# Second softmax attention of a three-mixer block in jobs of two banks, with three 64-row score products per head

## The reference, cut

```python
def sink_softmax(s, mask, sink):
    s = jnp.where(mask, s, NEG_INF)
    m = jnp.maximum(jnp.max(s, axis=-1, keepdims=True), sink)
    e = jnp.exp(s - m)
    return e / (jnp.sum(e, axis=-1, keepdims=True) + jnp.exp(sink - m))

def swa_sink_mixer(h, positions, w_in, q_gain, k_gain, sinks, w_out):
    ...
    q, k, v, z = jnp.split(h @ w_in, np.cumsum([MIX_WIDTH, kvd, kvd]).tolist(), axis=-1)
    q = q_groups(rope(rms_norm(split_heads(q, N_HEADS), q_gain), positions), g)
    k = jnp.pad(kv_groups(rope(rms_norm(split_heads(k, g), k_gain), positions)), pad)
    ...
    o = merge_blocks(lax.map(block_fn, jnp.arange(s // Q_BLOCK)))
    return (o * jax.nn.silu(z)) @ w_out
```

## Time and profile before

| | us |
|---|---|
| median of 3 runs (lowest, highest) | 844.62 (843.43, 844.91) |
| the profiled execution | 844.54 |
| its span, first to last instruction | 842.7 |
| PE busy | 801.4 (95%) |
| DVE busy | 561.2 (67%) |
| ACT busy | 429.0 (51%) |
| POOL busy | 113.6 (13%) |
| mean granted clock of TensorE | 0.993 of full speed |

### The profile page before, as it was taken

How to read it: one execution, slowest core, us unless ns; L and a number is a source line. 1 busy time by engine, 2 the same in 40 slices (tenths; PEclk the granted TensorE clock), 3 DMA queues, 4 the chain that set the end, 5 groups by cost and what they waited for, 6 DMA issues and landing times.

```text
span 842.7 us, 13226 instructions
## 1 busy us (share of the span) xinstructions
PE 801.4 (95%) x5114; PEld 698.4 (83%) x5114; DVE 561.2 (67%) x954; ACT 429.0 (51%) x838; POOL 113.6 (13%) x108
## 2 busy tenths in 40 slices
PE   5989999998889899999999999999999999999996
PEld 4768987776789678999988988889997788888885
DVE  5896977846887855346635657775875566566665
ACT  5436647825547544446536535555444445455453
POOL 2243214501532302000000000013001000000000
PEclk9999999999989999999999999999999999999999
DMA  9745411233442235544432534333654637655541
GB/s 313 214 154 170 136 51 35 68 124 111 149 151 101 75 101 174 177 150 149 152 101 85 166 104 146 101 101 100 225 174 129 217 131 234 227 174 190 186 164 51
DMA packets 93502, 121.38 MB, mean 144 GB/s; under 512 B 8760, under 2 KB 69616, under 8 KB 93440
## 3 DMA queue, kind: packets, MB, share of 16 engines
q1 hardware_dynamic: 92432, 117.80, 43.3%
q0 software_dynamic: 432, 1.57, 0.6%
q10 hardware_dynamic: 576, 1.17, 0.4%
HBM read 119.48 MB, written 1.05 MB: 143 GB/s over the span
## 4 chain that ended last, share of the span: by engine, by line
PE 79%; DVE 12%; issue 3%; ACT 1%; POOL 1%; POOLq 0%; DVEq 0%; ACTq 0%
PE banks L415 18%; PE banks L417 17%; PE banks L416 17%; PE banks L459 8%; PE banks L461 3%; DVE w_lo L1495 3%; PE banks L561 1%; DVE small L1589 1%; PE banks L617 1%; PE banks L945 1%; PE banks L422 1%; PE banks L421 1%; PE banks L575 1%; PE banks L520 1%; PE banks L555 1%
## 5 line engine op out<-in xcount | busy, mean ns | idle before, releaser
L1495 DVE TENSOR_TENSOR w_lo<-raw,w_hi 128x1024 fp32r<-128x1024 f32 x216 | 267.6, 1248 | 113.1 <-ACT w_hi L1092 111.1
L1092 ACT CAST w_hi<-raw 128x1024 fp32r<-128x1024 f32 (+1 forms) x217 | 225.2, 1045 | 155.6 <-PE banks L417 111.5
L415 PE MATMUL banks<-h,w_hi 128*128 128x256 f32 (+1 forms) x512 | 150.0, 293 | 2.9 <-DVE w_lo L1495 2.9
L416 PE MATMUL banks<-h,w_hi 128*128 128x256 f32 (+1 forms) x512 | 146.7, 286 | 0.0
L417 PE MATMUL banks<-h,w_lo 128*128 128x256 f32 (+1 forms) x512 | 145.7, 285 | 0.0
L415 PE MATMUL banks<-w_hi,h 128*128 128x512 f32 (+1 forms) x288 | 115.5, 401 | 11.6 <-DVE w_lo L1495 6.7
L417 PE MATMUL banks<-w_hi,h 128*128 128x512 f32 (+1 forms) x288 | 113.1, 393 | 0.0
L416 PE MATMUL banks<-w_lo,h 128*128 128x512 f32 (+1 forms) x288 | 112.8, 392 | 0.0
L415 PEld LDWEIGHTS banks<-h,w_hi 128*128 128x128 f32 x512 | 97.2, 190 | 7.3 <-issue 6.4
L459 PE MATMUL banks<-h,w_hi 128*128 128x512 f32 x288 | 99.1, 392 | 0.0
L417 PEld LDWEIGHTS banks<-h,w_lo 128*128 128x128 f32 x512 | 97.8, 191 | 0.0
(11 more groups left out here) (319 smaller groups left out, 1362.9 us busy)
## 6 DMA issues: line engine op xcount, KB each, us to landing
raw<-in_w_in SPq DMA_DIRECT2D x24, 1024.0 KB, 5.2
raw<-in_a_w_in SPq DMA_DIRECT2D x14, 1024.0 KB, 5.4
raw<-in_w_ffn_gate SPq DMA_DIRECT2D x11, 1024.0 KB, 5.4
raw<-in_w_ffn_up SPq DMA_DIRECT2D x11, 1024.0 KB, 5.4
raw<-in_w_ffn_down SPq DMA_DIRECT2D x11, 1024.0 KB, 5.0
raw<-in_b_w_in SPq DMA_DIRECT2D x9, 1024.0 KB, 5.3
raw<-in_w_gate SPq DMA_DIRECT2D x8, 1024.0 KB, 5.7
raw<-in_a_w_out SPq DMA_DIRECT2D x4, 1024.0 KB, 5.1
```

What stands on the lines that cost most here:

```text
L415: mm(o, lh, rh, start=start, stop=False)
L416: mm(o, lh, rl, start=False, stop=False)
L1092: nc.scalar.copy(split(w_hi, s), rawsub(s)[0]).then_inc(S["hi_ready"], 1)
L1495: V.tensor_tensor(split(w_lo, s), rawsub(s)[0], split(w_hi, s).bitcast(F), ALU.subtract).then_inc(S["lo_ready"], 1)
```

## The change

The second attention gets a loop of its own (`wide_attention`), and the first keeps the old one.

- **Products of 64 rows.** q is no longer stored as hi above lo. `o2_hi` and `o2_lo` hold it with two heads along the 128 rows, and the key lies twice as before. Each head takes three products of 64 rows (hi.hi, lo.hi, hi.lo) in place of two of 128. The heads of a pair use rows 0 to 63 and 64 to 127 and write to the two banks of a pair of banks, in turns.
- **Jobs of two banks.** Six jobs of 1024 columns (4 heads of tile 1, 4 more, 8 heads of tile 0, and again) in place of twelve of 512. Masks go to each bank. One maximum reduces both banks; ACT copies all transposed weights, DVE none. The lag between scores and transposes is 2 jobs, to the values 3. Weights go to three buffers of 1024 columns.
- **Moved into the loop.** The transposes and splits of the second half of q (heads 8 to 15) stand in iteration 0, behind the first job's scores and z3. Iterations 0 to 3 hold z4 to z7. The sub of z0 is cast by DVE before the first half of q is split, that of z1 right behind it. The first sub of the output projection (`out_first`) stands before the last job's values; for that the first two column panels of `b_out` are swapped, and banks 2 and 3 take subs 0 and 1.

```diff
...
-    def out_panels(name, m):
+    def out_panels(name, m, first=(0, 512)):
         v = m.rearrange("(a p) n -> p a n", p=P)
         for half in range(2):
-            for c0 in (0, 512):
+            for c0 in (0, 512) if half else first:
                 add(name, v[:, 4 * half:4 * half + 4, c0:c0 + 512], 4, 512, 2, "rows")
...
+    out_panels("b_out", w["b_w_out"], (512, 0))
...
+        p_buf = [ar[:, 8192:9216], ar[:, 9216:10240], tmp[:, 0:1024]]
...
+        WIDE = [(qt, tuple(range(b, b + n))) for a in range(0, NH, 8) for qt, b, n in ((1, a, 4), (1, a + 4, 4), (0, a, 8))]
+        LAGW = 2
...
+        def z_done_wide(j):
+            return 3 + min(max(j + 1, 0), 5)
...
+        def score_banks(j):
+            return pairs[1 - j % 2]
...
+        def quads_after(j):
+            return (2 * (j // 3), 2 * (j // 3) + 1) if 0 <= j < len(WIDE) and j % 3 == 2 else ()
...
+        def tbank(phase, e):
+            return ps[(6, 7, 4, 5, 4, 5)[e] if phase else (0, 1, 2, 3, 6, 7, 4, 5, 6, 7, 4, 5)[e]]
+        def z_bank(phase, f):
+            return ps[6 + f % 2 if phase and f >= 3 else f % 2]
...
-                        pe.wait_ge(S["tq_dve"], 8 + e - 3 if phase else e - 7)
+                        pe.wait_ge(S["tq_dve"], 12 if phase else e - 7)
...
+            def wide_attention(z0, s_out):
+                n = len(WIDE)
+                def scores(j):
+                    qt, heads = WIDE[j]
+                    w = P * (qt + 1)
+                    if j == 0:
+                        pe.wait_ge(S["rp_free"], 16)
+                    elif j == 1:
+                        pe.wait_ge(S["z_free"], 11)
+                    else:
+                        pe.wait_ge(S["p_exp"], NJ + 2 * j - 2)
+                    b = score_banks(j)
+                    nb = 4 // (qt + 1)
+                    for u in range(2):
+                        rows = b[:, u, :].rearrange("p (r n) -> p r n", n=w)
+                        mm(rows[:, :, w - P:w], tri, bc(far, [P, nb, P], 1), start=True, stop=True)
+                        if qt:
+                            mm(rows[:, :, 0:P], not_after, bc(far, [P, nb, P], 1), start=False, stop=False, skip_group_check=True)
+                    for q, k in ((o2_hi, k_hi), (o2_lo, k_hi), (o2_hi, k_lo)):
+                        for i in range(len(heads) // 2):
+                            for u in range(2):
+                                h, a = heads[2 * i + u], 64 * u
+                                last = mm(b[:, u, w * i:w * i + w], q[a:a + 64, h // 2, P * qt:P * qt + P],
+                                          k[a:a + 64, h // 8, 0, 0:w], start=False, stop=k is k_lo, skip_group_check=True)
+                    last.then_inc(S["s_ready"], 1)
...
+                def transposes(j):
...
+                    for u in range(2):
+                        pe.wait_ge(S["p_ready"], NJ + 2 * j + u + 1)
+                        if j:
+                            pe.wait_ge(S["pt_sb"], pt_wide(j - 1, u))
+                        for i in range(4):
+                            last = nc.tensor.transpose(ps[4 + u][:, P * i:P * i + P], p_buf[j % 3][:, 512 * u + P * i:512 * u + P * i + P], ident)
+                        last.then_inc(S["pt_ps"], 1)
...
+                def pv(j):
+                    qt, heads = WIDE[j]
+                    quad = heads[0] // 4
+                    pe.wait_ge(S["pt_sb"], pt_wide(j, 1))
+                    if j < 2:
+                        pe.wait_ge(S["z_free"], 15 + j)
+                    elif qt and quad >= 2:
+                        pe.wait_ge(S["og_ready"], 4 + quad - 1)
+                    for i in range(len(heads) // 2):
...
+                for j in range(n + LAGW + 1):
+                    if j < n:
+                        scores(j)
+                    if j == 0:
+                        z_tiles(1, z0, 3, 4)
+                        for tt in range(2):
+                            pe.wait_ge(S["rp_out"], 13 + tt)
+                            head_transposes(4 + tt, 1, q_half(tt, 1))
+                    if j < 4:
+                        z_tiles(1, z0, 4 + j, 5 + j)
+                    if j == 1:
+                        meta_transposes()
+                    if 0 <= j - LAGW < n:
+                        transposes(j - LAGW)
+                    if j == n + LAGW:
+                        pe.wait_ge(S["p_exp"], NJ + 2 * n - 2)
+                        out_first(s_out, 0)
+                    if j > LAGW:
+                        pv(j - LAGW - 1)
+                pe.wait_ge(S["p_exp"], NJ + 2 * n)
+            def out_first(s0, q):
+                if q < 2:
+                    pe.wait_ge(S["ot_lo"], 4 + q + 1)
+                weights_ready(s0 + q)
+                for j in range(2):
+                    last = tm_half(s0 + q, j, 2 * (q % 2) + j, hx(h_hi), hx(h_lo), (2, 3) if q < 2 else (0, 1), k_last=KT)
+                last.then_inc(S["sub_used"], 1)
...
+                    if n == 2:
+                        if q:
+                            out_first(s0, q)
+                        continue
...
-            z_tiles(1, first["b_z"], 1, 2)
-            for tt in range(2):
-                pe.wait_ge(S["rp_out"], 13 + tt)
-                head_transposes(4 + tt, 1, q_half(tt, 1))
-            z_tiles(1, first["b_z"], 2, 3)
-            pe.wait_ge(S["tq_dve"], 14)
-            attention(1, first["b_z"])
-            pe.wait_ge(S["z_free"], 16)
+            z_tiles(1, first["b_z"], 1, 3)
+            pe.wait_ge(S["tq_dve"], 12)
+            wide_attention(first["b_z"], first["b_out"])
...
+            def wide_attention(z0):
+                n = len(WIDE)
+                for j in range(n + LAGW + 3):
+                    if 1 <= j < 5:
+                        z_tanh(1, z0, 3 + j)
+                    v = j - LAGW
+                    if 0 <= v < n:
+                        for u in range(2):
+                            act.wait_ge(S["pt_ps"], NJ + 2 * v + u + 1)
+                            if v >= 2 and u == 0:
+                                act.wait_ge(S["pv"], NJ + v - 1)
+                            nc.scalar.copy(xn[:, 1024 * (v % 2) + 512 * u:1024 * (v % 2) + 512 * u + 512], ps[4 + u]).then_inc(S["pt_sb"], 1)
...
+                        act.wait_ge(S["s_max"], NJ + j + 1)
+                        if j >= 3:
+                            act.wait_ge(S["pt_ps"], NJ + 2 * j - 4)
...
+                    if j == 0:
+                        z_tanh(1, z0, 3)
+                        for i in range(2):
+                            q_hi_wide(4 + i, i, 1)
+                    for q in quads_after(j - LAGW - 2):
+                        output_hi(1, q)
+                    split_hi_to(z0 + z_done_wide(j) + RING)
...
+                def maxima(j):
+                    qt, heads = WIDE[j]
+                    nb, c = 4 // (qt + 1), 8 * (j % 4)
+                    dve.wait_ge(S["s_ready"], NJ + j + 1)
+                    m = nmax[:, c:c + 2 * nb]
+                    h = heads[0]
+                    by = lambda t: t[:, h:h + 2 * nb].rearrange("p (r u) -> p u r", u=2)
+                    of = lambda t: t.rearrange("p (u r) -> p u r", u=2)
+                    link(V.tensor_reduce(m, score_banks(j)[:, :, :].rearrange("p u (r n) -> p (u r) n", r=nb), X, ALU.max, negate=True))
+                    link(V.tensor_tensor(of(m), of(m), by(nsink), ALU.min))
+                    V.tensor_tensor(of(facs[:, 32 + c:32 + c + 2 * nb]), of(m), by(sink), ALU.add).then_inc(S["s_max"], 1)
...
+                    link(V.tensor_tensor(f, facs[:, 32 + c:32 + c + 2 * nb], sm_, ALU.add))
+                    V.reciprocal(f, f).then_inc(S["p_fac"], 1)
...
+                    if 1 <= j < 5:
+                        z_gate(1, 3 + j)
+                    if j == 0:
+                        z_gate(1, 3)
+                        for i in range(2):
+                            q_lo_wide(4 + i, i, 1)
+                        dve.wait_ge(S["m_rstd"], 1)
+                        V.tensor_scalar(meta_in, meta_in, m_st[:, 2:3], None, ALU.mult).then_inc(S["m_n"], 1)
...
+                    for q in quads_after(j - LAGW - 2):
+                        output_lo(1, q)
+                    if j == n:
...
+            split_lo_to(base + 3 + RING)
             for i in range(2):
-                q_lo(i, 12, 8 + i, i, 0)
-            split_lo_to(base + 5 + RING)
+                q_lo_wide(i, i, 0)
+            split_lo_to(base + 4 + RING)
...
-            dve.wait_ge(S["m_rstd"], 1)
-            V.tensor_scalar(meta_in, meta_in, m_st[:, 2:3], None, ALU.mult).then_inc(S["m_n"], 1)
+            rope_item(14, 15, 2, 8, 4, 0, q8(0, 1), 12)
+            z_gate(1, 0)
+            split_lo_to(base + RING - 1)
...
+                key_lo(2 + i, 1, 0, i, 2)
+            rope_item(15, 16, 3, 8, 4, 1, q8(1, 1), 13)
+            split_lo_to(base + RING)
             z_gate(1, 1)
-            for i in range(2):
-                q_lo(4 + i, 12, 12 + i, i, 1)
             split_lo_to(base + 2 + RING)
```

(5 more changed lines are left out.)

415 lines of the change are left out of this document (209 added, 206 removed).

## The result

The changed kernel takes **834.87 us** (834.01 to 835.61 in 4 runs) beside 844.76 us for the kernel before in the same comparison: a ratio of 0.9879, with a 95% interval of 0.9862 to 0.9896. It is faster by 1.2%, more than the 0.2% that can be told from no change. The forecast was 833.7 us, its range 831.0 to 839.5.

A forecast was written before the change was run, and what follows sets the result against it. PE's work and waits were taken to bound the kernel; in the stage from b_q2's last sub to the output projection, 5.2 + 0.3 + 2.5 + 3.8 + 3.4 - 4.4 = 10.8 us saved, 844.5 to 833.7; range 831.0 to 839.5.

The forecast's parts named there:

- Part 1: PE's wait before gate tile z0: the earlier cast saves 2.9 us waiting, 2.3 low clock; 0.3 more for low-clock transposes.
- Part 2: Second half of q: scores and z3 cover its rope and POOL, so waits of 1.7 and 0.8 go; 2.5 us saved.
- Part 3: PE's own work in the attention jobs: paired 64-row products and wider jobs take 21.6 us instead of 25.0; 3.4 saved.
- rival of serial pairs: Scores: the 64-row pairs run one after another, costing 5.4 us on PE's path; 839.1 us, chance 0.12.
- Part 4: Loop's tail: old waits of 3.8 us go; new ones before job 1's values and job 4's and 5's transposes cost 4.4.
- The third: In the tail, the new wait of PE before the transposes of job 5: 1.6 to 2 us.
- rival of the clock in the tail: From 270 us PE's three waits lower the clock, so first output subs run at half speed: 836.7 us, chance 0.12.

The follow-up runs named there:

- e8: Changed kernel with one more wait on PE ahead of gate tile z0, about 2.8 us at the old first wait's place: 839.19 us, ratio 0.9923 to before.
- e1: Changed kernel with DVE's cast of z0 put back behind the two splits of q: 836.36 us, ratio 0.9889 to the kernel before.
- e2: Kernel before with one edit only, the cast of z0 ahead of the four splits of q: 844.52 us, ratio 0.9987 to the kernel before.
- e7: Changed kernel with PE's transposes of q's second half back ahead of the first scores and z3: 838.18 us, ratio 0.9908 to the kernel before.
- e9: Changed kernel with every 64-row score product on rows 0 to 63, number and size kept: 841.53 us, ratio 0.9950 to the kernel before.
- e4: Changed kernel with DVE's gate of z7 ahead of the maxima of job 4: 835.22 us, ratio 0.9870 to the kernel before.
- e6: Changed kernel with DVE's factors of job 4 ahead of the maxima of job 5: 835.26 us, ratio 0.9877 to the kernel before.

## Why the prediction was right, and where not

The sum was 10.8 us; the stage gave 9.0. The forecast of 833.7 started from the profiled 844.54, and the profiled execution of the changed kernel took 835.6, 1.9 more than forecast. That the median is only 1.2 off is luck in part: two of its four executions were 1.5 us shorter. The direction, the places and most sizes held:

- **Part 1**, 5.2 + 0.3: the wait and the low clock are gone, and e8's profile confirms their price. The cause was wrong in part. I credited the moved cast; e1 shows that the cheaper splits alone leave only 0.8 of it. And the term was taken as independent, which e2 refutes.
- **Part 2**, 2.5: both waits are gone, and 0.68 before z3 came instead. I had named z3 the tightest, by 0.4, but put z2's cast at its quiet price. It took 1.90 beside POOL. e7's profile prices the part at 1.9. *Mis-sized: -0.7.*
- **Part 3**, 3.4: the rival of serial pairs is out (e9). But the jobs take 23.2 us, not 21.6. Scores of tile 1 take 246.84 - 245.37 = 1.47 to 1.57 (1.4 was put), of tile 0 2.14 (2.0); six groups 10.4 instead of 9.6. The transposes take 6.45 instead of 6.0 and the values 6.3 instead of 6.0, mostly for a first instruction behind a wait or a change of form. The 0.2 that I gave the change of form was an estimate, and too little: about 0.1 each for entering (the first product starts 245.94 - 245.73 = 0.21 us behind the last mask, where masks follow each other at 0.12), for the first pair (0.38 against 0.28 us) and for leaving (247.07 - 246.84 = 0.23 to the next start, where 0.12 is the pitch). *Mis-sized: -1.6, the largest error.*
- **Part 4**, old waits -3.8, new ones +4.4: they measure 1.37 (1.3 put), 1.08 + 0.34 (1.5), 0.83 + 0.52 (1.6 to 2), with 0.12 more before the values of job 0: 4.3. Right, although e4 and e6 show that they are not three costs but one chain: shortening the first gives 0.3 us, and taking the second away gives nothing or a loss. The third was put in the sum at its low end, 1.6, where its own terms give 7.6 - 5.5 = 2.1; it measured 1.35. That the old waits are gone is seen in the profile alone: no run put DVE's copies, or the first output sub, back in their old place.
- **The rest.** Of the 1.8 us missed, -0.7 and -1.6 are named above and +0.1 is the tail's. The other +0.4 lies in gate tiles and in the transposes of q and the meta tokens, which took 25.0 us together where 25.4 was put.
- **The rival of the clock in the tail** did not come about: 1.00 from 262 to 290 us, behind waits of up to 1.37. It was nearer than I thought, since in e6's profile it did (0.50), behind 2.53 us in one piece. In the profile of e7 PE waited 2.42 us between transposes and the clock stayed at 1.00, as it did in the tail with its transposes; no run took the transposes out, so it is not shown what they do to the clock.

## To carry to other kernels

A wait that is removed is worth only what the next supplier allows: before adding two gains, put the consumer forward by the first and ask each queue behind it whether it comes forward too (e2 took 2.9 us of wait away, and the stage stayed at 65.5). In a tail whose waits hang on one chain, remove the head of that chain (here a tanh on ACT behind a cast, and the gate on DVE that uses it), and don't gather short waits into one long one (in e6's profile the clock was 0.50 behind 2.53 us in one piece, in the changed kernel it was 1.00 behind four of 0.34 to 1.08). Price a DVE operation beside a POOL product at its collision, not at its quiet length (1.90 us for z2's cast, not 1.22).
